# Forming a feed-forward weight sum with a GpSimd pass on the chip, in place of a transfer that adds from memory

## The reference

```python
def swiglu(h, w1, w3, w2):
    return (jax.nn.silu(h @ w1) * (h @ w3)) @ w2
```

## Time and profile before

| | us |
|---|---|
| median of 2 runs | 951.82 (951.75 to 951.89) |
| span of the profiled execution, first to last instruction | 949.9 |
| TensorE busy | 942.9 |
| VectorE busy | 795.1 |
| ScalarE busy | 578.5 |
| GpSimd busy | 80.7 |

### The profile page before, as it was taken

The page is one execution under the profiler, slowest core; times in us unless marked ns, Lnnn a source line. Parts: engine busy times, 40 slices in busy tenths (PEclk is TensorE's granted clock), DMA queues, the critical chain, the costliest instruction groups (busy, mean ns, idle before and its releaser), DMA issues.

```text
span 949.9 us, 12049 instructions
## 1 busy us (share of the span) xinstructions
PE 942.9 (99%) x4719; PEld 786.6 (83%) x4719; DVE 795.1 (84%) x827; ACT 578.5 (61%) x611; POOL 80.7 (8%) x87
## 2 busy tenths in 40 slices
PE   8999999999999999999999999999999999999998
PEld 7878888888899888888888888888888888888887
DVE  5988999989866877999989887965885779999996
ACT  6566676576663655676666666565744456665672
POOL 3511101101000000101101021001010001101010
PEclk9999999999999999999999999999999999999999
DMA  8746888785464436879786365457255485987751
GB/s 303 263 134 210 245 305 226 203 284 133 153 223 136 155 112 220 244 252 258 199 280 163 116 219 182 171 182 218 93 198 196 164 275 139 318 236 208 256 133 45
DMA packets 125849, 191.14 MB, mean 201 GB/s; under 512 B 7256, under 2 KB 87520, under 8 KB 125792
## 3 DMA queue, kind: packets, MB, share of 16 engines
q1 hardware_dynamic: 110992, 172.59, 53.9%
q0 software_dynamic: 14496, 17.57, 10.5%
q10 hardware_dynamic: 304, 0.20, 0.1%
HBM read 189.29 MB, written 1.05 MB: 200 GB/s over the span
## 4 chain that ended last, share of the span: by engine, by line
PE 99%; DMA 0%; ACT 0%; issue 0%; DVE 0%; ACTq 0%
PE psum L2149 27%; PE psum L2150 26%; PE psum L2154 26%; PE psum L2293 4%; PE psum L2142 2%; PE psum L2144 2%; PE psum L2143 2%; PE psum L2684 1%; PE psum L2695 1%; PE psum L2685 1%; PE psum L2310 1%; PE psum L2718 1%; PE psum L2334 1%; PE psum L2746 1%; PE psum L2493 0%; DMA gains<-in_norm_mix_g 0%
## 5 line engine op out<-in xcount | busy, mean ns | idle before, releaser
L1399 DVE TENSOR_TENSOR low<-raw,high 128x2048 fp32r<-128x2048 f32 (+1 forms) x109 | 245.3, 2252 | 60.1 <-ACT high L849 60.1
L849 ACT ACTIVATE high<-raw 128x2048 fp32r<-128x2048 f32 (+1 forms) x112 | 211.6, 1890 | 83.8 <-PE psum L2154 69.1
L2149 PE MATMUL psum<-high,xh 128*128 128x512 f32 x596 | 237.1, 398 | 0.0
L2150 PE MATMUL psum<-high,xl 128*128 128x512 f32 x596 | 232.6, 390 | 0.0
L854 ACT ACTIVATE high<-arena 128x2048 fp32r<-128x2048 f32 x88 | 168.7, 1917 | 76.3 <-PE psum L2154 72.1
L1405 DVE TENSOR_TENSOR low<-arena,high 128x2048 fp32r<-128x2048 f32 x88 | 200.5, 2284 | 11.1 <-ACT high L854 11.1
L2154 PE MATMUL psum<-low,xh 128*128 128x512 f32 x596 | 155.4, 390 | 0.0
L2149 PEld LDWEIGHTS psum<-high,xh 128*128 128x128 f32 x596 | 112.0, 188 | 23.3 <-issue 0.7
L2154 PEld LDWEIGHTS psum<-low,xh 128*128 128x128 f32 x596 | 111.7, 188 | 23.6 <-issue 0.3
L2150 PEld LDWEIGHTS psum<-high,xl 128*128 128x128 f32 x596 | 112.0, 188 | 22.0
L2149 PE MATMUL psum<-high,mh 128*128 128x512 f32 x256 | 102.1, 399 | 0.0
(11 more groups left out here) (252 smaller groups left out, 1183.8 us busy)
## 6 DMA issues: line engine op xcount, KB each, us to landing
raw<-in_ffn_w SPq DMA_DIRECT2D x68, 512.0 KB, 6.5
arena<-in_ffn_w SPq DMA_DIRECT2D x64, 512.0 KB, 7.5
raw<-in_w_in SPq DMA_DIRECT2D x50, 512.0 KB, 4.6
raw<-in_od_w_qkv SPq DMA_DIRECT2D x24, 512.0 KB, 4.6
raw<-in_w_ffn_down SPq DMA_DIRECT2D x22, 512.0 KB, 6.4
arena<-in_ffn_w POOLq DMA_DIRECT2D x16, 512.0 KB, 7.5
arena<-in_w_ffn_gate SPq DMA_DIRECT2D x16, 512.0 KB, 6.5
arena<-in_w_ffn_up SPq DMA_DIRECT2D x16, 512.0 KB, 8.2
```

The source lines that it names most:

```text
L849: nc.scalar.activation(high[:, n % RING, 0:cols], raw[:, r, 0:cols], ACT.Copy).then_inc(high_ready, 1)
L1399: nc.vector.tensor_tensor(low[:, n % RING, 0:cols], raw[:, RING_AT[n] % RING, 0:cols], high[:, n % RING, 0:cols].bitcast(F32), ALU.subtrac ...
L2149: nc.tensor.matmul(out, sh, wh, start=start, stop=False, skip_group_check=True)
L2150: nc.tensor.matmul(out, sl, wh, start=False, stop=False, skip_group_check=True)
```

## The change

`weight_sums` no longer issues two transfers that read the second-half weight rows from memory again and add them to the b12 block. It waits until X22, which holds the same numbers, is in SBUF, and adds X22 to the b12 block with one GpSimd instruction. The semaphore counts one instruction in place of 32 transfer parts. SyncE waits for it before it loads the next pair's X22.

```diff
                 def load_x22(p):
                     low_is_made("P", pair_before(p), 3)
+                    sp.wait_ge(t3_made, pair_seq(f, pair_before(p)) + 1)
                     up_quarter(f, X22, p + 1, 1, x22_in)
...
             def weight_sums(f):
                 for p in PAIRS:
                     pool.wait_ge(t_ready, sums_made(f, p, 1))
-                    block = b12_block(p).rearrange("p (k c) -> p k c", k=4)
-                    for j in range(2):
-                        src = FFN_W[f][j][4 * P:D, (p + 1) * FC:(p + 2) * FC]
-                        pool.dma_start(block[:, :, j * FC:(j + 1) * FC], src.rearrange("(k p) c -> p k c", p=P), accum_op=ALU.add
-                                       ).then_inc(t3_in, 16)
+                    pool.wait_ge(x22_in, 32 * pair_seq(f, p) + 32)
+                    nc.gpsimd.tensor_tensor(b12_block(p), b12_block(p), X22, ALU.add).then_inc(t3_made, 1)
...
                     if i == 7:
-                        act.wait_ge(t3_in, 32 * pair_seq(f, p) + 32)
+                        act.wait_ge(t3_made, pair_seq(f, p) + 1)
```

More of the change, by code:

```diff
@@ L411, in program @@
         x_copied = sem("x_copied")
-        t_ready, t3_in, prep_step, rbc_ready = sem("t_ready"), sem("t3_in"), sem("prep_step"), sem("rbc_ready")
+        t_ready, t3_made, prep_step, rbc_ready = sem("t_ready"), sem("t3_made"), sem("prep_step"), sem("rbc_ready")
         diag_ready = sem("diag_ready")
```

## The result

The changed kernel takes 988.47 us (987.24 to 989.70, 2 runs) against 951.82, a ratio of 1.038 (95% interval 1.035 to 1.042). It is slower by 36.7 us; 31.6 us more were forecast (983.4), and 988.5 lies in the range of 960 to 1002.

The account below looks back on a forecast made before the run. TensorE was taken as the bound, busy 942.9 of 949.9 us; VectorE stops from GpSimd's pass reach it as 10.5 us per feed-forward, 3 x 10.5 = 31.6 us, plus 1.9 us to the runs' median: 983.4 us, range 960 to 1002.

Parts of the forecast that it names:

- What is removed: Two GpSimd-issued transfers and about 1 MB of reading for each of 12 pairs; TensorE waits for none, so worth 0.
- The pass's own time and the new waits: Twelve GpSimd passes of 4.58 us, wanted late, and SyncE's added wait before the next X22 load: each costs 0.
- The stops: Each GpSimd pass holds up one VectorE two-input instruction: 3.7, 4.15, 3.5, 3.7 us in pairs 2, 4, 7, 9.
- a row of 1.26 us: VectorE two-input instruction issued at 31.60 beside a 1.35 us GpSimd pass; its like took 0.34, so stopped about 0.9 us.
- when both read two SBUF blocks: Claimed rule: VectorE and GpSimd then exclude each other for whole instructions, and the one that started first keeps the other out.
- the prediction's own row at 695.56: GpSimd instruction of 0.19 us that takes 2.14 us when issued behind a VectorE two-input instruction ending at 697.65.
- The way to TensorE: How much of VectorE's lag reaches TensorE, through the smallest spare times: 10.5 us for each of three feed-forwards.
- T: Lag of TensorE, rising where its need comes soonest after VectorE's work: 2.85, 6.05, 8.0, 10.5 us in pairs 2, 4, 7, 9.
- V: Lag of VectorE, falling only where VectorE idled and never below T: 3.7, 7.85, 9.25, 11.7 us in pairs 2, 4, 7, 9.
- the four places: Tightest points before TensorE: product 3's low part, pair 4's gate, pair 7's transposed hidden low part, pair 9's gate; 0.86, 1.82, 1.24, 1.17 us spare.
- rival C: TensorE's clock falls for 10 us after each of 12 pauses of 2 to 3 us, 5 us each: 1043 us; chance 0.03.
- if the granted clock falls: Last listed sign that the forecast is wrong; TensorE's granted clock was 1.00 in each profiled stretch before the change.

Follow-up runs that it names:

- eight columns: Changed kernel with the GpSimd pass cut to the first 8 of 2048 columns, all waits kept and the transfers still missing: 951.74 us.
- the transfer on the chip: Changed kernel with the GpSimd pass replaced by one GpSimd-issued transfer a pair that adds X22 to the block from SBUF: 951.67 us.
- eight pieces: Changed kernel with the GpSimd pass cut into eight instructions of 256 columns each: 973.14 us.
- the memset: Changed kernel with the GpSimd pass replaced by a GpSimd memset of the same block, which writes and reads nothing: 951.82 us.
- one-input run: Changed kernel with the GpSimd pass replaced by one with a single SBUF input, X22 times 1 into the block: 973.16 us.
- pair 2 alone: Changed kernel with the GpSimd pass only in pair 2 of each feed-forward, the other pairs adding from memory as before: 962.94 us.
- on VectorE: Changed kernel with the sum made by one VectorE instruction a pair, right behind t2, and no GpSimd pass: 965.23 us.
- four pieces: Changed kernel with the GpSimd pass cut into four instructions of 512 columns each: 971.62 us.
- pair 4 alone: Changed kernel with the GpSimd pass only in pair 4 of each feed-forward, the other pairs adding from memory as before: 958.91 us.

## Why the prediction was right, point by point

- **What is removed is worth 0.** Shown by eight columns and by the transfer on the chip: both read 176.7 MB and take the time before.
- **The pass's own time and the new waits cost 0.** Shown by eight columns. In no run with one whole pass a pair does TensorE wait for ScalarE or for a weight load, and ScalarE's waits in the changed kernel don't name GpSimd's sum. The sum is late only with eight pieces.
- **The stops.** Forecast 3.7, 4.15, 3.5 and 3.7 us, measured 3.83, 3.94, 3.54 and 3.82, from a row of 1.26 us for a pass less than a third as long. The reason given for them was right in its main part (reads against reads: the memset does nothing). One part was too narrow: "when both read two SBUF blocks". One input on GpSimd is enough, as the one-input run shows, and as the prediction's own row at 695.56 did: `L829` multiplies and adds constants to a single input. One part was too simple: "until 0.2 us before its end" holds for the two-input pass and not for the one-input pass, which let VectorE go 1.9 us before its end.
- **The way to TensorE.** T was to grow by 2.85, 3.2, 1.95 and 2.5 us. The start of t1 in each pair shows the lag. The changed kernel's timeline of VectorE, then the one before:

```profile
103.88 2.28 DVE L1571 TENSOR_TENSOR arena<-arena 128x2048 f32<-128x2048 f32 x1
...
143.68 2.28 DVE L1571 TENSOR_TENSOR arena<-arena 128x2048 f32<-128x2048 f32 x1
```

```profile
104.21 2.28 DVE L1573 TENSOR_TENSOR arena<-arena 128x2048 f32<-128x2048 f32 x1
...
140.19 2.28 DVE L1573 TENSOR_TENSOR arena<-arena 128x2048 f32<-128x2048 f32 x1
```

  From 104.21 to 140.19 are 35.98 us, from 103.88 to 143.68 are 39.80: V is 3.8 before pair 4 (forecast 3.7). At the gl of pair 7 TensorE paused 1.8 us (forecast 1.95) and at the gate of pair 9 2.6 (forecast 2.5). The pauses came at the kinds of places named: low parts, gl, gates. T at the four places was 4.0, 6.1, 8.1 and 11.0 for 2.85, 6.05, 8.0 and 10.5.
- **The sum was not complete.** It had 31.6 us of waits and no clock. The span grew by 38.0: 24.4 us of waits, some 10.5 of slower clock and 3 of friction at the pauses. The step that failed is rival C's dismissal, "nothing in the rows speaks for it", which was true of the rows and yet no reason. The last of the prediction's own signs of being wrong, "if the granted clock falls", came true. It happened in small: six falls of 1.7 us where the rival had twelve of 5. They cost less than 10 us, because a fall slows TensorE and not VectorE: behind pair 2 TensorE was 1.15 us later than forecast, V was still 3.8, and pair 4 then added 2.1 us in place of 3.2. In each feed-forward one fall stayed in the sum with some 1.7 us, and T at the last gate was 0.5 us over the forecast. So by an estimate from these shifts the clock is 5 of the 6.4 us by which the span grew more than forecast. The stops and the spare times were near what was measured (the first without a fall is 3.2 us for 2.85, by pair 2 alone), and that the missing clock didn't cost more is luck.
- **Small slips.** 7.85 less 1.82 is 6.03, not 6.05, and the chances above 971 us add to 0.79, not 0.78. Neither matters.
- **VectorE's extra busy time** was put at 45 us, and is 45.1.

Open is what ties the fall of the clock to a pause. The pause's length alone doesn't: of the nine pauses of 1.8 us and more in the changed kernel's feed-forwards six had a fall and three had none, with equal lengths on both sides. In the traces whose longest pause behind the first wait is 1.6 us or less (one input, on VectorE, four pieces, pair 4 alone) the clock is 1.000. No run varied the pause by itself. Also open is why the one-input pass lets VectorE go 1.9 us before its end.

## What to carry to other kernels

Work given to GpSimd isn't free because GpSimd is idle: a pass that reads SBUF shuts out VectorE's two-input instructions, here for 3.8 of 4.6 us with two inputs and 2.9 of 5.4 us with one. So 2.2 us of VectorE's own work became 3.8 us of standing. Before such a move, look for one row where both engines meet, and for the smallest spare time between the stopped engine and the one that sets the end. Where only the memory traffic is to be saved, a transfer that adds from SBUF to SBUF did it here without slowing any engine, and where a pass must stay, pieces of a quarter cost half as much here.

## What the runs showed of the hardware

- A GpSimd pass with one input took longer (5.37 us) than one with two (4.62) over the same 128x2048 block, and stopped VectorE for less (2.85 against 3.83 us in pair 2).
- A GpSimd memset of 128x2048 (1.82 us) beside a two-input VectorE instruction lengthened neither.
- At six of nine pauses of 1.8 to 2.6 us TensorE went down to 1.2 GHz for some 3.4 us in this kernel, for a loss of 1.7 us of work each time, though it was busy nearly all of the time around them. The other three had none, and traces with no pause over 1.6 us show no fall.
- A GpSimd-issued transfer of 1 MB from SBUF to SBUF that adds landed in 7.9 us (median of 12), and VectorE was not slowed by it: it is busy 795.2 us in that run, 795.1 before.
